# Reordering the steps between the two products of a convolution block: last transform by token halves, normed values ahead of an inverse transform, a gate sum in halves, a silu written rounded

## The reference, cut to what matters

```python
def conformer_conv(h, w_pw1, b_pw1, w_dw, b_dw, ln_g, ln_b, w_pw2, b_pw2):
    a = h @ w_pw1 + b_pw1                                  # 1024 -> 2048
    u = a[..., :D_MODEL] * jax.nn.sigmoid(a[..., D_MODEL:])
    u = depthwise_causal_conv(u, w_dw, 31 taps) + b_dw     # along the 256 tokens
    u = layer_norm(u, ln_g, ln_b)                          # over the 1024 channels
    return jax.nn.silu(u) @ w_pw2 + b_pw2                  # 1024 -> 1024
```

## Time and profile before

| | |
|---|---|
| median of 3 runs | 1201.41 us (1200.98, 1201.41, 1202.93) |
| the profiled execution, its own time | 1202.96 us |
| its span | 1201.2 us |
| TensorE busy | 1188.8 us, 99% of the span |
| VectorE / ScalarE / GpSimd busy | 916.0 (76%) / 674.5 (56%) / 174.4 us (15%) |
| DMA queue of the weights | 50.4% of 16 engines |
| mean granted TensorE clock | 0.998 of full speed |

### The profile page before, as it was taken

How to read it: one execution, slowest core, us unless ns; L and a number is a source line. 1 busy time by engine, 2 the same in 40 slices (tenths; PEclk the granted TensorE clock), 3 DMA queues, 4 the chain that set the end, 5 groups by cost and what they waited for, 6 DMA issues and landing times.

```text
span 1201.2 us, 14347 instructions
## 1 busy us (share of the span) xinstructions
PE 1188.8 (99%) x5556; PEld 979.0 (82%) x5556; DVE 916.0 (76%) x1147; ACT 674.5 (56%) x810; POOL 174.4 (15%) x171
## 2 busy tenths in 40 slices
PE   8999999999999999999999999999999999999997
PEld 7777888888888888888888888888888888888886
DVE  7677798878678898878788878655577666988884
ACT  6665666556547565555565555545434545666552
POOL 2400132120200132120031220000000000322200
PEclk9999999999999999999999999999999999999999
DMA  8424465556432655555455555645544454555540
GB/s 338 175 105 167 149 236 190 183 205 256 147 141 75 223 197 186 197 210 196 156 198 187 210 211 179 274 170 209 180 171 142 155 194 154 199 202 183 186 180 36
DMA packets 32759, 220.71 MB, mean 184 GB/s; under 512 B 3777, under 2 KB 4305, under 8 KB 7090
## 3 DMA queue, kind: packets, MB, share of 16 engines
q1 hardware_dynamic: 32546, 219.59, 50.4%
q10 hardware_dynamic: 144, 0.20, 0.0%
HBM read 218.72 MB, written 1.05 MB: 183 GB/s over the span
## 4 chain that ended last, share of the span: by engine, by line
PE 95%; DVE 1%; POOL 1%; ACT 1%; issue 1%; DMA 0%; SPq 0%; POOLq 0%; DVEq 0%
PE ps L259 29%; PE ps L261 29%; PE ps L260 29%; PE ps L264 4%; PE ps L267 4%; POOL st L395 1%; POOL AR L898 0%; DMA raw<-in_w 0%; ACT whi L228 0%; DVE wlo L218 0%; ACT whi L211 0%; DVE st L1738 0%; DVE h L406 0%; SPq L2530 0%; DVE AR L2508 0%
## 5 line engine op out<-in xcount | busy, mean ns | idle before, releaser
L218 DVE SCALAR_TENSOR_TENSOR wlo<-raw,whi 128x2048 fp32r<-128x2048 f32 x160 | 367.6, 2301 | 122.6 <-ACT whi L211 92.5
L259 PE MATMUL ps<-whi,xh 128*128 128x512 f32 x1104 | 435.8, 395 | 0.0
L261 PE MATMUL ps<-whi,xl 128*128 128x512 f32 x1104 | 430.4, 390 | 0.0
L260 PE MATMUL ps<-wlo,xh 128*128 128x512 f32 x1104 | 430.0, 389 | 0.0
L211 ACT CAST whi<-raw 128x2048 fp32r<-128x2048 f32 x162 | 310.0, 1914 | 182.5 <-PE ps L261 180.9
L259 PEld LDWEIGHTS ps<-whi,xh 128*128 128x128 f32 x1104 | 207.2, 188 | 48.1 <-issue 1.7
L261 PEld LDWEIGHTS ps<-whi,xl 128*128 128x128 f32 x1104 | 207.2, 188 | 44.7
L260 PEld LDWEIGHTS ps<-wlo,xh 128*128 128x128 f32 x1104 | 207.4, 188 | 40.7
L259 PE MATMUL ps<-whi,yh 128*128 128x512 f32 x344 | 137.9, 401 | 0.0
L261 PE MATMUL ps<-whi,yl 128*128 128x512 f32 x344 | 134.4, 391 | 0.0
L260 PE MATMUL ps<-wlo,yh 128*128 128x512 f32 x344 | 134.0, 389 | 0.0
(11 more groups left out here) (240 smaller groups left out, 1224.5 us busy)
## 6 DMA issues: line engine op xcount, KB each, us to landing
raw<-in_w SPq DMA_DIRECT2D x198, 1024.0 KB, 4.8
raw<-in_w SPq DMA_DIRECT2D x4, 512.0 KB, 7.8
h<-in_x SPq DMA_DIRECT2D x4, 256.0 KB, 5.2
raw<-in_w SPq DMA_DIRECT2D x4, 256.0 KB, 4.7
AR<-in_b_pw SPq DMA_DIRECT2D x1, 1024.0 KB, 4.7
AR<-in_gate_bias SPq DMA_DIRECT2D x1, 1024.0 KB, 7.0
AR<-in_dft SPq DMA_DIRECT2D x1, 864.0 KB, 8.9
AR<-in_rmask SPq DMA_DIRECT2D x1, 768.0 KB, 8.6
```

The lines of the kernel that those rows point to most:

```text
L218: e.scalar_tensor_tensor(out=wlo[:, v % S, :], in0=raw[:, v % R, :], scalar=1.0, in1=whi[:, v % S, :].bitcast(F32), op0=ALU.mult, op1=ALU. ...
L259: e.matmul(o, ah, bh, start=start, stop=False, skip_group_check=skip)
L260: e.matmul(o, ah, bl, start=False, stop=False, skip_group_check=skip)
L261: return e.matmul(o, al, bh, start=False, stop=stop, skip_group_check=skip)
```

## The change

Six edits, all in the convolution.

1. The bias sum of the last (j, t) = (3, 1) is two instructions of 256 columns, the gate half first; the sigmoid waits for that half only (`last_gate`), the product for both.
2. `tensor_last_forward` takes the place of `tensor_forward(2)`. It works per token half and per set of frequency parts, and does all products with the high part of `u` before it waits for the low part. Half 0, parts 0 and 1, now runs ahead of the inverse (0, 0); then half 1, parts 0 and 1; then part 2 of both halves.
3. `tensor_normed(0, 0)`, the transposes of the first 512 normed channels, stands ahead of the inverse (2, 1) instead of behind it.
4. The first silu, (0, 1), is computed twice from PSUM: straight into the rounded `yh`, and then into `act` unrounded. The rounding copy is gone. The remainder waits for both.
5. ScalarE rounds parts 0 and 1 of group 1 before the last sigmoid (before: part 0 only). VectorE does the imaginary products of group 1 before the last bias sum, the third one before the last gate product, and two of the three remainders of group 1 before the last `ul`.
6. The four quarters of `lo(u + 8)` move: number 1 from before the gate product (3, 0) to between the moments and the shift of half 1, number 2 from there to behind the remainder (0, 1).

```diff
@@ -1590,12 +1590,21 @@
-    e.scalar_tensor_tensor(out=glu[:, t, :], in0=ps[4 + t][:, :], scalar=rstd[:, t:t + 1],
-                           in1=bp1[:, 512 * j:512 * j + 512], op0=ALU.mult,
-                           op1=ALU.add).then_inc(*banks.empty("pw1", j, t))
+    if (j, t) == (3, 1):
+        e.scalar_tensor_tensor(out=glu[:, t, 256:512], in0=ps[4 + t][:, 256:512], scalar=rstd[:, t:t + 1],
+                               in1=bp1[:, 512 * j + 256:512 * j + 512], op0=ALU.mult,
+                               op1=ALU.add).then_inc(*sig.up("last_gate", 0))
+        e.scalar_tensor_tensor(out=glu[:, t, 0:256], in0=ps[4 + t][:, 0:256], scalar=rstd[:, t:t + 1],
+                               in1=bp1[:, 512 * j:512 * j + 256], op0=ALU.mult,
+                               op1=ALU.add).then_inc(*banks.empty("pw1", j, t))
...
 
 def vector_glu_product(e, q, j, t):
     q.wait_ge(*sig.at("glu_sig", j, t))
+    q.wait_ge(*banks.emptied("pw1", j, t))
     e.tensor_tensor(glu[:, t, 0:256], glu[:, t, 0:256], glu[:, t, 256:512],
                     ALU.mult).then_inc(*sig.up("glu_out", j, t))
...
 def scalar_glu(e, q, j, t):
-    q.wait_ge(*banks.emptied("pw1", j, t))
+    q.wait_ge(*(sig.at("last_gate", 0) if (j, t) == (3, 1) else banks.emptied("pw1", j, t)))
...
+def tensor_last_forward(e, q, t, ms):
+    at, n = CH[2]
+    at_ = slice(at, at + n)
+    q.wait_ge(*sig.at("u_hi", 3, t))
+    for m in ms:
+        b, c0, group = freq_at(2, m)
+        first = m == 0 or freq_at(2, m - 1)[2] != group
+        if t == 0 and first:
+            banks.take(b, "freq", 2, group)
+            q.wait_ge(*banks.room("freq", 2, group))
+            q.wait_ge(*sig.at("fl", 0))
+        f0, w = MS[m]
+        mm(e, ps[b][0:w, c0:c0 + n], fh[:, t, f0:f0 + w], uh[:, t, at_], t == 0 and first, False, skip=True)
+        mm(e, ps[b][0:w, c0:c0 + n], fl[:, t, f0:f0 + w], uh[:, t, at_], False, False, skip=True)
+    q.wait_ge(*sig.at("u_lo", 3, t))
+    for m in ms:
+        b, c0, group = freq_at(2, m)
+        f0, w = MS[m]
+        last = mm(e, ps[b][0:w, c0:c0 + n], fh[:, t, f0:f0 + w], ul[:, t, at_], False, t == 1, skip=True)
+    if t == 1:
+        last.then_inc(*banks.full("freq", 2, group))
...
-def vector_freq(e, q, c):
-    for m in range(3):
+def vector_freq(e, q, c, parts=(0, 1, 2)):
+    for m in parts:
         hi_, lo_, src = freq_part(c, m)
         q.wait_ge(*sig.at("freq_hi", c, m))
         e.tensor_tensor(lo_, src, hi_.bitcast(F32), ALU.subtract).then_inc(*sig.up("freq_lo", c, m))
...
+    if (t, c) == (0, 1):
+        for g in range(2):
+            q.wait_ge(*banks.filled("freq", 2, g))
+        for k in (0, 1):
+            d = e.activation(yh[:, k, tcols(0)], ps[b][:, P * k:P * k + P], ACT.Silu, scale=parm("ln_g", k),
+                             bias=parm("ln_b", k))
+        d.then_inc(*sig.up("act_hi", 0, 1))
+        for k in (0, 1):
+            d = e.activation(act[:, k, tcols(0)], ps[b][:, P * k:P * k + P], ACT.Silu, scale=parm("ln_g", k),
+                             bias=parm("ln_b", k))
+        d.then_inc(*sig.up("first_act", 0))
+        return
...
 def vector_remainder(e, q, t, c):
     w = (slice(None), slice(c - 1, c + 1), tcols(t))
     q.wait_ge(*sig.at("act_hi", t, c))
+    if (t, c) == (0, 1):
+        q.wait_ge(*sig.at("first_act", 0))
     e.tensor_tensor(yl[w], act[w], yh[w].bitcast(F32), ALU.subtract).then_inc(*sig.up("act_lo", t, c))
...
+    tensor_last_forward(e, q, 0, (0, 1))
     q.wait_ge(*sig.at("gl", 0))
     tensor_inverse(e, q, 0, 0)
-    tensor_forward(e, q, 2)
+    tensor_last_forward(e, q, 1, (0, 1))
+    tensor_last_forward(e, q, 0, (2,))
+    tensor_last_forward(e, q, 1, (2,))
     tensor_inverse(e, q, 0, 1)
     tensor_inverse(e, q, 1, 0)
     tensor_inverse(e, q, 2, 0)
     tensor_inverse(e, q, 1, 1)
+    tensor_normed(e, q, 0, 0)
     tensor_inverse(e, q, 2, 1)
-    tensor_normed(e, q, 0, 0)
     tensor_normed(e, q, 0, 1)
...
         else:
-            scalar_freq(e, q, 1, (0,))
+            scalar_freq(e, q, 1, (0, 1))
             scalar_glu(e, q, 3, 1)
-            scalar_freq(e, q, 1, (1, 2))
+            scalar_freq(e, q, 1, (2,))
...
     vector_freq(e, q, 0)
     vector_glu_sum(e, q, 3, 0)
     lo_quarter(e, q, u + 8, 0)
-    lo_quarter(e, q, u + 8, 1)
     vector_glu_product(e, q, 3, 0)
     vector_real(e, q, 1)
     vector_glu_low(e, q, 3, 0)
+    vector_imag_first(e, q, 1)
+    vector_imag(e, q, 1)
     vector_glu_sum(e, q, 3, 1)
-    vector_imag_first(e, q, 1)
+    vector_third(e, q, 1)
     vector_glu_product(e, q, 3, 1)
-    vector_imag(e, q, 1)
+    vector_freq(e, q, 1, (0, 1))
     vector_glu_low(e, q, 3, 1)
-    vector_third(e, q, 1)
-    vector_freq(e, q, 1)
+    vector_freq(e, q, 1, (2,))
     vector_stats(e, q, 0, 0)
     vector_products(e, q, 2)
     vector_freq(e, q, 2)
@@ -1940,9 +1990,10 @@
     vector_stats(e, q, 1, 2)
     vector_stats(e, q, 1, 3)
     vector_moments(e, q, 1)
-    lo_quarter(e, q, u + 8, 2)
+    lo_quarter(e, q, u + 8, 1)
     vector_shift(e, q, 1)
     vector_remainder(e, q, 0, 1)
+    lo_quarter(e, q, u + 8, 2)
     lo_quarter(e, q, u + 8, 3)
     lo_quarter(e, q, u + 9, 0)
     vector_remainder(e, q, 0, 3)
```

More of the change, by code:

```diff
@@ L1592, in vector_glu_sum @@
             q.wait_ge(*sig.at("rstd", "mix1", t))
-            e.scalar_tensor_tensor(out=glu[:, t, :], in0=ps[4 + t][:, :], scalar=rstd[:, t:t + 1],
-                                   in1=bp1[:, 512 * j:512 * j + 512], op0=ALU.mult,
-                                   op1=ALU.add).then_inc(*banks.empty("pw1", j, t))
+            if (j, t) == (3, 1):
[5 more added lines that the diff above has]
+                                       op1=ALU.add).then_inc(*banks.empty("pw1", j, t))
+            else:
+                e.scalar_tensor_tensor(out=glu[:, t, :], in0=ps[4 + t][:, :], scalar=rstd[:, t:t + 1],
+                                       in1=bp1[:, 512 * j:512 * j + 512], op0=ALU.mult,
+                                       op1=ALU.add).then_inc(*banks.empty("pw1", j, t))
         def vector_glu_product(e, q, j, t):
             q.wait_ge(*sig.at("glu_sig", j, t))
+            q.wait_ge(*banks.emptied("pw1", j, t))
             e.tensor_tensor(glu[:, t, 0:256], glu[:, t, 0:256], glu[:, t, 256:512],
```

## The result

The changed kernel takes 1204.53 us (median of 13 runs, 1202.87 to 1205.31) against 1201.97 (13 runs, 1200.97 to 1203.12) for the kernel before. The ratio, taken from all runs, is 1.0018, 95% interval 1.0010 to 1.0025: 2.2 us slower, just inside the 0.2% that the prediction called no change. The two medians lie 2.56 us apart, and the interval reaches past 0.2%, so what can be said is that it is slower, by 1.2 to 3.0 us.

The account below looks back on a forecast made before the run. TensorE, busy 99% of the span, bounds the kernel. Upstream gains of 0.34 and an earlier pw2, then later waits, net 1.4 us: 1201.41 + 1.4 = 1202.8 us, range 1200.8 to 1204.8.

Parts of the forecast that it names:

- R2: Rival, 25%: TensorE's clock falls around its two stalls, costing 1.6 us on top of 1.4, giving 1204.4 us.
- the prediction's own sign: In the changed kernel's profile, a granted clock below 1.00 between 372 and 386 us would mean the clock-fall rival.
- Upstream gain of 0.34: VectorE's group 2 products start 1.0 us earlier; 0.34 reaches inverse (2, 0), as rounding copies wait for inverse (0, 1).
- Transposes ahead of the inverse (2, 1): TensorE idles 1.9 us before the first transposes; pw2 is ready 1.96 us after they can start, at 377.62.
- The remainder behind the shift: On VectorE, remainder (0, 1) starts 1.70 us after half 1's statistics; TensorE's second pw2 round stands 1.55 us.
- The quarters: Two `lo(u + 8)` quarters behind remainder (0, 1) finish at 381.15; pw2's third round starts at 381.30, another 0.2 us late.
- The sum of 1.4: After pw2's third round the next transposes come at 382.25 instead of 380.86, 1.4 us later, kept to the end.
- T0: Time when TensorE can start the first transposes of normed values: 375.66 us instead of 376.00.
- R1: Rival, 12%: remainder (0, 1) is not held back, pw2 gains 0.43 us, up to 0.9 in all; time 1201.0 us.
- the silu's wait: TensorE's 1.17 us wait between the first transposes and pw2, expected to vanish with pw2 starting 0.43 us earlier.
- R3: Rival, 13%: upstream gains and downstream waits cancel, or edits bring nothing; within 0.5 us of before, 1201.4 us.
- the base of three runs: Median of three runs of the kernel before, 1201.41 us, to which the forecast added its 1.4 us.

Follow-up runs that it names:

- own buffers: Changed kernel with the transposes back behind inverse (2, 1), group 2 in separate buffers, inverse (0, 1) split, VectorE and ScalarE reordered: ratio 0.9994 to the kernel before.
- the clock held up: Changed kernel plus 12 unread matmuls of 256 columns in TensorE's idle time before the first transposes: median 1202.76 us, ratio 1.0014 to the kernel before.
- queues turned: Changed kernel with VectorE's remainder (0, 1) ahead of the shift, `lo` quarters moved, ScalarE's silu (0, 3) ahead of half 1's normed values: ratio 1.0012 to before.

## Why the prediction was right, and where it was short

The forecast was 1202.8 with 1.0 to 1.7 us over the kernel before; 1204.53 and 2.32 us in the trace (2.56 between the medians) lie above both. The measured time is inside the stated range only because that range was drawn to hold R2. By the prediction's own sign, a granted clock below 1.00 between 372 and 386 us, it is R2 that happened: the forecast was right in its path and short of one term.

1. *Upstream gain of 0.34.* 0.32 at the inverse (2, 0), 0.33 at the first transposes. Its reason holds too: 0.96 us earlier products, 0.53 us of VectorE's wait for the copies, and the version with own buffers and a split inverse (0, 1), where the copies wait for no matmul, starts its transposes another 0.61 earlier.
2. *Transposes ahead of the inverse (2, 1).* 1.9 us idle forecast; in the issue of matmuls 371.74 + 0.12 to 373.69, 1.83. Right, and shown as the cause from both sides.
3. *The remainder behind the shift.* Forecast 1.70 from the end of the statistics (376.77 in this trace) to its start at 378.48: 1.71. GpSimd's power took 0.93 as assumed, with a quarter of `lo` started 0.17 before it; no run left the quarter out, so why it takes longer than the 0.55 of half 0 is not tested. That the remainder's place costs the time is shown by turning the queue.
4. *The quarters.* The third round starts 1.20 after the second, forecast 381.30 - 380.09 = 1.21; without a wait it is 0.91.
5. *The sum of 1.4.* With the clock held up it is 1.39. The measured total is 2.32, and the step that failed is in the terms of point 2: transposes, the inverse (2, 1) and the first round were taken at full pace ("four transposes (0.44), the inverse (2, 1) (1.07)", pw2 ready at T0 + 1.96). They took 376.81 - 373.69 = 3.12. The fall of the clock stood among the rivals, as R2 with 25% and 1.6 us; it came, and cost 0.93. The price was too high as all the lost speed was counted. 1.70 us were lost in the windows, but only the inverse (2, 1) is on the path to the statistics and so to the remainder, and it took 2.03 instead of 1.15: 0.88. The rest was lost in the transposes and the first round, while TensorE would only have reached the wait for the remainder sooner: that wait was 0.63 idle, and 1.28 with the clock held up (1.55 forecast).
6. *R1* fell: the silu's wait did go, yet the start of pw2 was later, not earlier. *R3* fell with the interval's lower end, 1.0010: 1.2 us, where it allowed 0.5.

R2 deserved more than 25%: the 1.9 us of idle time was forecast in full, right beside a row of the same trace where a sparse stretch was followed by 0.61. Its number, 3.0 over the base, would have been off by 0.7 in the trace, the chosen 1.4 by 0.9. That its time, 1204.4, is within 0.2 us of the measured median is partly luck: 3.0 was too much, and the base of three runs, 1201.41, was 0.56 below the median of 13.

## What to carry to other kernels

Where one engine bounds and stands still in several small places, moving a piece of its work from one wait to the next does not shorten the sum, and everything that reads the moved piece becomes late: list who reads it, and what is queued behind that reader on its own engine. Before a wait of the bounding engine is made longer, look for what its clock did after a similar stretch elsewhere in the trace; two half waits can be cheaper than one whole. An earlier start upstream is worth only what the next wait lets through, so look for buffer reuse that ties a copy to a matmul. And a gain of a few tenths read from one stretch has to be followed through the stages behind it: the 2.3 us of edit 3 last to the end here, the 0.3 of edit 6 and the 0.2 of edit 4 do not.

## What the runs showed of the hardware

The first microseconds of this kernel decide some 2 us of its time, and the ten profiles, of kernels that do not differ there, show where. In seven the last matmul of pw1 starts at 361.76 to 362.54 us, in three at 363.71 to 364.03. These three (before, queues turned, own buffers) are the ones in which the granted clock from 8 to 12 us is low: 0.61, 0.63 and 0.57, against 1.00 in the seven (above for the changed kernel). From 4 to 8 us TensorE was busy 2.08, 2.19 and 1.97 us of four in them, and 2.90 to 3.48 in the others. The delay is there by GpSimd's first power: 18.39 to 18.72 us in the three, 16.51 to 17.28 in the seven. So a sparse start, a fallen clock behind it and the later time go together in all ten; no run forced the start one way or the other, and what makes it sparse in one execution and not in the next is not shown.

It does mean that here a single total can hide or feign 2 us: with edit 3 taken back, eleven runs took 1200.66 to 1203.95 us. A change of 0.3 us is read from a stretch of the trace, and from the stages behind it, or not at all.
